# Mixture-of-experts encoder layer: the combine of the previous expert moved between the second and third up group, and one more load split into single slabs

## What is computed

```python
def moe_ffn(h, w_router, b_router, w_up, b_up, w_down, b_down):   # N=256 tokens, D=1024, 32 experts
    logits = (t @ w_router + b_router)
    top_val, top_idx = lax.top_k(logits, 4); gates = jax.nn.softmax(top_val, axis=-1)
    # for every expert e, on the tokens that chose it:
    up = xb @ w_up[e] + b_up[e]                                   # 1024 -> 2048
    glu, lin = up[:, :1024], up[:, 1024:]
    glu = jnp.minimum(glu, 7.0); lin = jnp.clip(lin, -7.0, 7.0)
    act = glu * jax.nn.sigmoid(1.702 * glu) * (lin + 1)
    y_e = act @ w_down[e] + b_down[e]                             # 1024 -> 1024
    # out[token] += gate * y_e[token]
```

## Time and profile before

| | |
|---|---|
| median of 3 runs | 1141.87 us (1141.70 to 1141.93) |
| profiled execution | 1140.42 us |
| its span, first to last instruction | 1138.7 us |
| TensorE (PE) busy | 1115.0 us, 98% of the span |
| VectorE (DVE) / ScalarE (ACT) / GpSimd (POOL) busy | 362.1 / 215.7 / 84.7 us |
| mean granted TensorE clock | 0.997 |
| moved by DMA | 437.62 MB, 384 GB/s over the span |

### The profile page before, as it was taken

One profiled execution on the slowest core, in us unless ns is written; L12 is line 12 of the kernel. 1 busy time (PEld: TensorE's weight loads), 2 busy tenths in 40 slices (PEclk: granted clock), 3 DMA queues, 4 the chain that ended last, 5 costly groups with the idle time before them and its releaser, 6 DMA issues.

```text
span 1138.7 us, 15628 instructions
## 1 busy us (share of the span) xinstructions
PE 1115.0 (98%) x5248; PEld 483.5 (42%) x5249; DVE 362.1 (32%) x909; ACT 215.7 (19%) x401; POOL 84.7 (7%) x206
## 2 busy tenths in 40 slices
PE   8999999999999999999999999999999999999998
PEld 6786487543333333333333333333333333333344
DVE  5899413232322222222222332222222222222223
ACT  5312212121111112111111111111111111111113
POOL 1991000000000000000000000000000000000000
PEclk9999999999999999999999999999999999999999
DMA  9566336489999999999999999999999999999996
GB/s 363 195 259 268 147 148 257 186 363 431 430 435 425 437 428 433 433 432 432 429 436 426 439 427 436 429 432 432 430 435 426 439 427 437 428 425 427 425 424 262
DMA packets 29115, 437.62 MB, mean 384 GB/s; under 512 B 4064, under 2 KB 4704, under 8 KB 12320
## 3 DMA queue, kind: packets, MB, share of 16 engines
q1 hardware_dynamic: 28224, 436.10, 90.4%
q10 hardware_dynamic: 864, 1.14, 0.3%
HBM read 436.18 MB, written 1.05 MB: 384 GB/s over the span
## 4 chain that ended last, share of the span: by engine, by line
PE 84%; DMA 14%; SPq 0%; another core or an unknown queue 0%; issue 0%; DVE 0%; ACT 0%; ACTq 0%; DVEq 0%
PE bank L1841 35%; PE bank L1870 16%; DMA ring<-in_w_up_dram 13%; PE total L1802 5%; PE bank L1789 4%; PE bank L1465 2%; PE bank L1484 2%; PE bank L1878 2%; PE bank L1698 2%; PE bank L1475 2%; PE bank L1796 1%; PE bank L1631 1%; PE total L1631 1%; DMA ring<-in_w_in_dram 1%; PE bank L1996 1%; PE bank L1590 1%
## 5 line engine op out<-in xcount | busy, mean ns | idle before, releaser
L1841 PE MATMUL bank<-ring,buf_m 128*64 128x512 f32 (+1 forms) x2160 | 464.5, 587 | 12.6 <-DMA ring<-in_w_up_dram 12.6
L1841 PEld LDWEIGHTS bank<-ring,buf_m 128*64 128x64 f32 x2160 | 158.2, 138 | 313.1 <-issue 307.0
L1870 PE MATMUL bank<-ring,buf_f 128*64 128x512 f32 x1024 | 232.2, 595 | 0.0
L1353 DVE COPY buf_f<-bank 128x512 f32<-128x512 f32 x32 | 22.1, 692 | 445.7 <-PE bank L1841 445.7
L1870 PEld LDWEIGHTS bank<-ring,buf_f 128*64 128x64 f32 x1024 | 67.9, 136 | 136.1 <-issue 115.0
L884 ACT ACTIVATE buf_f<-buf_f 128x256 f32<-128x256 f32 x32 | 13.3, 416 | 331.7 <-DVE buf_f L1363 331.7
L1802 PE MATMUL total<-buf_m,wr_sb 64*128 64x512 f32 x264 | 65.6, 615 | 0.7 <-ACT buf_m L891 0.7
L1789 PE MATMUL bank<-buf_k,buf_m 128*64 128x512 f32 x264 | 63.9, 605 | 0.0
L650 POOL TENSOR_TENSOR buf_m<-table,buf_m 128x4 f32<-128x4 f32 x33 | 6.6, 199 | 762.7 <-DVE channel_vecs L1340 762.0
L1359 DVE TENSOR_TENSOR buf_f<-bank,buf_m 128x512 f32<-128x512 f32 x64 | 44.0, 687 | 57.8 <-PE bank L1878 57.8
L891 ACT ACTIVATE buf_m<-bank 128x512 f32<-128x512 f32 x32 | 19.1, 598 | 185.3 <-PE bank L1870 185.3
(11 more groups left out here) (386 smaller groups left out, 844.3 us busy)
## 6 DMA issues: line engine op xcount, KB each, us to landing
ring<-in_w_up_dram SPq DMA_DIRECT2D x48, 4096.0 KB, 33.2
ring<-in_w_down_dram SPq DMA_DIRECT2D x24, 4096.0 KB, 31.7
ring<-in_w_up_dram SPq DMA_DIRECT2D x29, 2048.0 KB, 15.8
ring<-in_w_down_dram SPq DMA_DIRECT2D x12, 2048.0 KB, 13.6
ring<-in_w_down_dram SPq DMA_DIRECT2D x7, 1024.0 KB, 36.4
ring<-in_w_up_dram SPq DMA_DIRECT2D x6, 1024.0 KB, 36.9
ring<-in_w_in_dram SPq DMA_DIRECT2D x4, 1024.0 KB, 17.1
ring<-in_w_xkv_dram SPq DMA_DIRECT2D x2, 2048.0 KB, 27.2
```

Source lines behind the costliest of these rows:

```text
L1841: ins = t_.matmul(banks[bank][h * 64:(h + 1) * 64, c0:c1], xg[:, k, :], w[:, :, k % 4, h, :], start=first, stop=last)
L1870: ins = t_.matmul(banks[2][h * 64:(h + 1) * 64, :], actT[:, f, :], group(p, UPS + f // 4)[:, lo + h * BANK:lo + (h + 1) * BANK], start=f = ...
```

## The change

On PE the combine moves in the block of every expert 0 to 30: from behind the fourth up group to between the second and the third, with its waits (in a function of its own, `add_last_y`). `last_expert` stays as it is. On SP the third up group of expert 30 is loaded in two single slabs, as its fourth was; `up_late` now serves both groups, so the products of the third are issued in halves of 256 columns as well, each half behind its own slab. No semaphore count of PE that SP waits for changes its meaning: `up_steps` is incremented after each group as before.

```diff
--- before.py
+++ after.py
@@ -372,7 +372,7 @@
         zeroed = sem("first_combine_zeroed")
         last_up_in = [[sem(f"last_up_quarter{2 + q}_inputs{k}_in") for k in range(2)] for q in range(2)]
         last_down_in = [sem(f"last_down_part{h}_rows_from_{f}_in") for h, f in LAST_DOWN]
-        late_up_in = sem("third_up_quarter_of_last_but_one_in")
+        late_up_in = [sem(f"first_half_of_up_group_{i}_of_last_but_one_in") for i in (2, 3)]
         late_down_in = [sem(f"down_rows_from_{4 * i}_of_last_but_one_in") for i in range(DOWNS)]
         last_y = sem("last_expert_y_part_scaled")
         last_up = sem("last_expert_up_piece_full")
@@ -510,8 +510,8 @@
                 n2 = last_block(e - 2)
                 for i in range(UPS):
                     sp.wait_ge(up_steps, n2 * UPS + (i + 1))
-                    if e == E - 2 and i == UPS - 1:
-                        load_slab(up_v, e, p, i, i, 0, late_up_in)
+                    if e == E - 2 and i >= UPS // 2:
+                        load_slab(up_v, e, p, i, i, 0, late_up_in[i - UPS // 2])
                         load_slab(up_v, e, p, i, i, 1, slabs_in[p][i])
                     else:
                         load_up(e, p, i)
@@ -1852,15 +1852,16 @@
                                       i % 2 == 1 and k == 3)
                 ins.then_inc(up_steps, 1)
 
-            def up_late(p):
+            def up_late(p, i):
 
                 for q in range(2):
                     if q == 0:
-                        pe.wait_ge(late_up_in, 16)
+                        pe.wait_ge(late_up_in[i - 2], 16)
                     else:
-                        pe.wait_ge(slabs_in[p][UPS - 1], transfers_into(E - 2, UPS - 1) * 16)
-                    for k in range(4, KT):
-                        ins = up_products(quarters(p, UPS - 1)[:, q:q + 1], 1, q * 256, (q + 1) * 256, k, False, q == 1 and k == KT - 1)
+                        pe.wait_ge(slabs_in[p][i], transfers_into(E - 2, i) * 16)
+                    for k in range(4 * (i % 2), 4 * (i % 2) + 4):
+                        ins = up_products(quarters(p, i)[:, q:q + 1], 1, q * 256, (q + 1) * 256, k, k == 0 and q == 0,
+                                          q == 1 and k == KT - 1)
                 ins.then_inc(up_steps, 1)
 
             def down_block(p, f):
@@ -1877,6 +1878,14 @@
                 for f in range(4 * c, 4 * c + 4):
                     ins = t_.transpose(banks[2 + c][:, f % 4 * P:(f % 4 + 1) * P], U_sb[:, f * P:(f + 1) * P], ident[:, :])
                 ins.then_inc(t_full, 1)
+
+            def add_last_y(at, n):
+
+                pe.wait_ge(y_ready, n + 1)
+                pe.wait_ge(pt_copied, n + 1)
+                if at == 0:
+                    pe.wait_ge(loaded["bdown"], 32)
+                combine()
 
             def expert(e, at, turns=0, rounds=None):
 
@@ -1894,17 +1903,14 @@
                             pe.wait_ge((xg_half, xg_ready)[i], n + 1)
                         if i == 2:
                             pe.wait_ge(pt_copied, n + 1)
-                        if (at, i) == (E - 2, UPS - 1):
-                            up_late(p)
+                        if i == 2:
+                            add_last_y(at, n)
+                        if at == E - 2 and i >= 2:
+                            up_late(p, i)
                         else:
                             wait_in(i)
                             up_group(p, i)
 
-                    pe.wait_ge(y_ready, n + 1)
-                    pe.wait_ge(pt_copied, n + 1)
-                    if at == 0:
-                        pe.wait_ge(loaded["bdown"], 32)
-                    combine()
                     pe.wait_ge(u_by_a, n + 1)
                     up_columns(0)
                     pe.wait_ge(u_by_v, n + 1)
```

## The result

| | before | after |
|---|---|---|
| median | 1141.90 us, 6 runs (1140.41 to 1143.52) | 1145.87 us, 6 runs (1144.92 to 1147.15) |
| profiled execution | 1140.42 us | 1146.65 us |
| its span | 1138.7 us | 1145.0 us |
| mean granted TensorE clock | 0.997 | 0.998 |

The ratio after to before is 1.004, 95% interval 1.003 to 1.005: 3.4 to 5.7 us slower. The forecast was 1142.8 us and the range ended at 1145.2. What happened is nearest to rival 1, a larger stall (1146.0 us).

The account below looks back on a forecast made before the run. The stream of weights was taken to set the time. Slip +0.95, tail -0.15 and split +0.1 gave +0.9 us, so the median of 1141.87 became 1142.8 us; the range was 1141.2 to 1145.2.

Parts of the forecast that it names:

- rival 1: Larger stall per block, say 0.6 us, from slow restart or late copy: 4.2 us of slip, 1146.0 us; chance 0.16.
- The bound: From expert 23 on, the gapless stream of weights sets the time; PE has 0.3 us slack at the last down piece.
- the forecast's 17.6 us: PE's waits in experts 23 to 30 and their consequences, room for the stalls of 32 blocks (11.2 us).
- The stall: Second four transposes in each block wait for VectorE's copy of bank 1, no longer covered by the combine: 0.35 us.
- the row of the restart: Last expert: a copy ends at 1120.67, transposes start at 1120.72; this 0.05 us restart was used to price the stall.
- The slip behind expert 11: Load behind expert 11's second round issued 4.55 us later, queue runs empty, whole stream slips by 0.95 us.
- the reserve of 3.6 us: Margin of the load issued at 583.65: 15.8 us to landing less 12.2 us for 4 MB into an empty queue.
- gain of 2.4 us of margin per later expert: Loads after those behind expert 11's second round gain 2.4 us of margin per expert and are safe.
- The load of groups 2 and 3: Issued at 571.0 with 6.5 us in hand, uses 6.1; the combine's extra 1.92 us do not decide.
- The tail: Expert 30's fourth group ends some 2 us sooner; of 0.3 us at expert 31's last down piece, 0.15 counted as gain.
- the split: Expert 30's third up group as two 1 MB pieces for one 2 MB transfer: costs 0.1 us, bounds 0 to 0.5.
- the clock: Forecast: stays at 2.4 GHz; rival 3: falls to 1.2 GHz in the last expert, costing 1.74 us, 1144.5 us, chance 0.05.

Follow-up runs that it names:

- e2: Changed kernel with the combine moved only in experts 12 to 30; 1140.54 us against 1141.40 for the kernel before, ratio 1.000.
- e3: Changed kernel with the combine moved only in experts 0 to 11, split kept; 1145.40 us against 1141.40 for the kernel before, ratio 1.0044.
- e7: Kernel before with the one-hot transposes done twice per block (0.22 us more), combine not moved; 1141.78 us against 1141.17, ratio 1.0004.
- e8: Kernel before with the one-hot transposes done four times per block (0.66 us more), combine not moved; 1147.24 us against 1141.17, ratio 1.0050.
- e6: Changed kernel with the combine moved only in experts 28 to 30, split kept; 1141.69 us against 1141.40 for the kernel before, ratio 1.0003.
- e1: Kernel before with only expert 30's third up group loaded and used in single slabs; 1140.83 us against 1141.40, ratio 1.000.
- e4: Changed kernel with the one-hot transposes put between the first and second four transposes; 1142.27 us against 1141.17 for the kernel before, ratio 1.0007.
- e5: Changed kernel with experts 12 to 15 loaded in 2 MB groups, their loops written out; 1144.06 us against 1141.17 for the kernel before, ratio 1.0025.

## Why the prediction was wrong

- **The bound** was read rightly. The stream decides from about 300 us on, and stalls of 11.0 us in the experts behind the second round are free (e2). That this ends at the forecast's 17.6 us was not tried.
- **The stall, the step that failed.** The forecast took 0.35 us, "from the row of the restart". That row, a wait for ScalarE's copy, priced the start of the second four transposes to 0.01 us (0.87 measured where 0.86 was said); the first four cover 0.49 of it and not 0.51, so this part is 0.38. Left out was what the move does to TensorE's own sequence: two runs of up products instead of one, +0.15, and 0.05 behind the start of the second four transposes. Together they make 0.58 us. The forecast counted each group of products at its own length and asked for no row on what lies between two shapes. The bounds given (0 to 0.86) held the value; the value chosen was too small.
- **Rival 1** named the chain from a larger stall to the slip, and the point (0.46 us) from which it decides. The reasons it gave for a larger stall, a slow restart or a late copy, were mostly not what happened. It was given 0.16 because the row for it was explained by the copy's length. That its 1146.0 us lies 0.1 us from the median is partly luck: its slip is 4.2 us where the landings show 5.2, and with the fall of the clock taken off the change costs 4.8 us and not 4.0.
- **The slip behind expert 11** was placed rightly (e2 against e3), but the reserve of 3.6 us was sized too large, a second and smaller failure: 13 x 0.58 - 3.6 = 3.9 us, and the trace shows 5.2 to 5.3. With a stall of 0.22 us the formula gives no slip, and e7's landings show 0.8. The first load into the empty queue took 12.1 us, where 12.2 was said. The Trainium skill (DMA: Bandwidth & Descriptors, Anatomy of one DMA) gives 2.0 us plus bytes over 436 GB/s for a DMA that GpSimd issues, an estimated 11.6 for 4 MB; the loads here, which SP issues, took 12.0 to 12.1. But the forecast took 12.2 as enough for the down load too, which comes about 2 us before the load ahead of it lands (issued at 592.6; the load ahead lands 13.1 us after 581.5, at 594.5): it took 13.7 (13.1 in e3, 13.4 in e8). The short queue is paid for twice, and it is paid for before it is empty. The prediction's gain of 2.4 us of margin per later expert should read 2.8, its own 29.1 - 26.36; nothing hangs on it.
- **The load of groups 2 and 3** landed 9.9 us behind the load ahead of it, where before it was 9.7: it lost 0.2 us. In e8, where no combine stands ahead of that load, it lost nothing; so the combine's 1.92 us cost some 0.2 us here, near the nothing that was said.
- **The tail** did nothing that can be measured (e6), nor did the split (e1), and the clock stayed at 2.4 GHz in the experts, as said: 0.98 over 880 to 1000 us before, 1.00 after. The waits for weights shrank further than forecast (2.7 us instead of 7): there are 32 x 0.58 = 18.6 us of stalls in their place, where 11.2 were forecast.
- **Ways back.** Cover for the stall (e4), moving only from expert 12 on (e2) and narrow loads (e5) all lose less than the change; none is faster than the kernel before beyond its interval, since the stream sets the end and they can at best leave it where it was.

## What to carry to other kernels

When a piece of work is moved on an engine, price both seams: what stops being covered, and what the piece now cuts in two; the extra change of matmul shape (0.15 us) was two fifths as large as the exposed copy (0.38). When a stream is the bound, look for the one place where its queue runs low and divide the time in hand by the number of iterations before it: here some 3.6 us over 13 blocks, 0.28 us a block. Treat it as a slope and not as a free allowance: 0.22 us a block already let the landings slip by 0.8 us, and 0.58 by 5. Before a loop is written out in a kernel bound by DMA, look at the queue of instruction fetches.

## What was not expected of the hardware

- A 4 MB load issued 1.6 to 2.0 us before the one ahead of it has landed took 13.1 to 13.7 us, and landed 11.1 to 11.7 us behind it; one that found the queue empty took 12.0 to 12.1 us. Issued 2.3 us before, it landed 10.6 us behind; issued 3.1 to 4.0 us before, 9.7 to 10.5 behind; issued 5.2 us or more before, 9.7. Why was not tried; that some of the 16 DMA engines are idle before the last of them is done would fit, but is only argued.
- Seven more program fetches of 16 KB went with 1.4 us (0.6 to 2.6) on a full stream. In the trace two of the seven delay it, by 0.4 and 1.1 us, several times the time of their bytes, and five do not.
- One more change of matmul shape in a block goes with about 0.15 us of TensorE (13.98 against 13.83 us for the 64 up records).
- The fall of the clock before the experts, 1.45 us in the changed kernel's profile, is in five profiles of eleven, so profiles of two kernels can differ by it alone.
